# The mixer of a two-block fp32 model: one activation table set for exponential and logarithm, output maps ahead of head 0's sum, three copies on ScalarE, unread matmuls taken out

## The reference, cut to what matters

```python
# branch 1: a diagonal complex state-space model ("s5"), 32 groups of 16 channels, 64 states each
a_bar = exp(lam * dt)
bu = einsum('bsgc,gpc->bsgp', ug, b_bar)          # complex
states = scan(x_t = a_bar * x_{t-1} + bu_t)
y = Re(C states) + D_skip * u                     # later: gelu, gated linear unit
# branch 2: stick-breaking attention, 8 heads of 64
z = q.k / 8                                        # masked to s < t
log_fail = log_sigmoid(-z)                         # = -(max(z, 0) + log(1 + exp(-|z|)))
log_w = log_sigmoid(z) + (sum of log_fail between s and t)
w = exp(log_w);  out = w @ v
```

## Time and profile before

| | us |
|---|---|
| median of 3 runs | 1498.22 (1497.93 to 1499.45) |
| the profiled execution's own time | 1497.39 |
| its span, first to last instruction | 1495.6 |
| from the first chunk's `in_transposes` to the fourth's | 54.77 to 205.07 |
| busy in the span: PE, DVE, ACT | 1414.9, 955.8, 703.5 |

### The profile page before, as it was taken

How to read it: one execution, slowest core, us unless ns; L and a number is a source line. 1 busy time by engine, 2 the same in 40 slices (tenths; PEclk the granted TensorE clock), 3 DMA queues, 4 the chain that set the end, 5 groups by cost and what they waited for, 6 DMA issues and landing times.

```text
span 1495.6 us, 18290 instructions
## 1 busy us (share of the span) xinstructions
PE 1414.9 (95%) x7056; PEld 1190.4 (80%) x7056; DVE 955.8 (64%) x1333; ACT 703.5 (47%) x932; POOL 75.6 (5%) x82
## 2 busy tenths in 40 slices
PE   4899999999999999999979999999999999996996
PEld 3788887888888888888868889787878888885875
DVE  6898886444554444444469776546888778886474
ACT  4677767332342223222246444435456666565251
POOL 3000000000110000000020000020100000000211
PEclk9999999999999999999988999999999999997997
DMA  5111011322222232222311211322312111111211
GB/s 196 57 57 57 1 57 57 113 85 89 108 85 102 96 112 85 97 99 85 110 63 54 84 56 60 124 85 85 116 56 82 56 56 56 56 60 67 85 57 56
DMA packets 19242, 118.22 MB, mean 79 GB/s; under 512 B 2401, under 2 KB 3681, under 8 KB 5617
## 3 DMA queue, kind: packets, MB, share of 16 engines
q1 hardware_dynamic: 18896, 116.38, 21.8%
q0 software_dynamic: 288, 1.05, 0.2%
HBM read 115.32 MB, written 2.10 MB: 79 GB/s over the span
## 4 chain that ended last, share of the span: by engine, by line
PE 76%; DVE 13%; ACT 8%; issue 2%; DMA 0%; DVEq 0%; ACTq 0%
PE ps L508 23%; PE ps L510 23%; PE ps L509 23%; DVE wlo L1637 2%; PE ps L975 1%; PE ps L698 1%; PE ps L944 1%; DVE att L1894 1%; DVE acc L384 1%; ACT att L1217 1%; PE ps L579 1%; DVE atlo L1898 1%; PE ps L962 1%; ACT att L1215 1%; ACT att L1213 1%
## 5 line engine op out<-in xcount | busy, mean ns | idle before, releaser
L508 PE MATMUL ps<-uhi,whi 128*128 128x512 f32 x1104 | 442.5, 401 | 8.4 <-DVE ulo L1698 3.0
L510 PE MATMUL ps<-uhi,wlo 128*128 128x512 f32 x1104 | 433.1, 392 | 0.0
L509 PE MATMUL ps<-ulo,whi 128*128 128x512 f32 x1104 | 432.9, 392 | 0.0
L1637 DVE TENSOR_TENSOR wlo<-wraw,whi 128x2048 fp32r<-128x2048 f32 x105 | 243.5, 2321 | 103.1 <-ACT whi L1088 101.6
L1088 ACT ACTIVATE whi<-wraw 128x2048 fp32r<-128x2048 f32 x105 | 200.3, 1908 | 178.8 <-PE ps L510 178.4
L508 PEld LDWEIGHTS ps<-uhi,whi 128*128 128x128 f32 x1104 | 209.3, 190 | 56.6 <-issue 9.6
L510 PEld LDWEIGHTS ps<-uhi,wlo 128*128 128x128 f32 x1104 | 209.3, 190 | 45.4
L509 PEld LDWEIGHTS ps<-ulo,whi 128*128 128x128 f32 x1104 | 209.6, 190 | 43.6 <-issue 1.9
L508 PE MATMUL ps<-hdhi,whi 128*128 128x512 f32 x256 | 99.6, 389 | 0.0
L509 PE MATMUL ps<-hdlo,whi 128*128 128x512 f32 x256 | 99.6, 389 | 0.0
L510 PE MATMUL ps<-hdhi,wlo 128*128 128x512 f32 x256 | 99.6, 389 | 0.0
(11 more groups left out here) (405 smaller groups left out, 2484.1 us busy)
## 6 DMA issues: line engine op xcount, KB each, us to landing
wraw<-wstream SPq DMA_DIRECT2D x105, 1024.0 KB, 4.8
h<-xT SPq DMA_DIRECT2D x4, 512.0 KB, 5.7
outT<-pp SPq DMA_DIRECT2D x8, 256.0 KB, 2.2
s5b<-s5p_d SPq DMA_DIRECT2D x1, 1024.0 KB, 12.0
pe_in<-pT POOLq DMA_DIRECT2D x2, 512.0 KB, 3.8
cst_in<-cst_d SPq DMA_DIRECT2D x5, 64.0 KB, 10.1
reset<-cst_d SPq DMA_DIRECT2D x1, 256.0 KB, 11.1
ones<-cst_d SPq DMA_DIRECT2D x1, 64.0 KB, 2.1
```

The costliest lines, as they stand in the source:

```text
L508: nc.tensor.matmul(out, lh, rh, start=start, stop=False, skip_group_check=True)
L509: nc.tensor.matmul(out, lh, rl_, start=False, stop=False, skip_group_check=True)
L510: mm = nc.tensor.matmul(out, ll, rh, start=False, stop=stop, skip_group_check=True)
L1637: V.tensor_tensor(wlo[:, slot, :], wraw[:, slot, :], whi[:, slot, :], ALU.subtract).then_inc(lo_done, 1)
```

## The change

Four edits, all in the mixer:

1. `table` ends with an explicit load of the set that holds both exponential and logarithm. No other ACT_TABLE_LOAD stands between it and the next chunk's Sin.
2. `tokens`, the copy of y into `tT` (now `y_tokens`) and `decays` go from VectorE to ScalarE. Their waits and the semaphores that they signal stay the same.
3. `out_maps` comes first in VectorE's part of a chunk, with three independent passes at its head; `blocks` stands inside it, behind the fourth pass.
4. `keep_on` and its twelve matmuls a chunk are gone.

```diff
@@ TensorE
-            def keep_on(n, bank, moving):
-                for _ in range(n):
-                    nc.tensor.matmul(ps[:, bank, :], identr[:, :], moving, start=True, stop=True)
...
                 gemm(n, 0, one(0), 256, uhi, ulo)
                 block_sums()
-                keep_on(12, 1, uhi[:, 0, :])
                 log_weights(0)
@@ ScalarE
                 A(cosT[:, :, :], cosT[:, :, :], ACT.Sin, scale=-TWO_PI, bias=halfpi_b).then_inc(table_ready, 1)
+                nc.scalar.preload_act_table_set("natural_log_exp_and_others")
+            def tokens(i):
+                act.wait_ge(u_tr, i + 1)
+                copy(tT[:, :, :].rearrange("p q (j c) -> p j q c", j=L),
+                     ps[:, 1, :].rearrange("p (j q c) -> p j q c", j=L, q=QP)).then_inc(u_tok, 1)
+            def y_tokens(i):
+                act.wait_ge(y5_done, i + 1)
+                copy(tT[:, :, :].rearrange("p b (q c) -> p q b c", q=QP),
+                     ps[:, 6, :].rearrange("p (q b c) -> p q b c", q=QP, b=L)).then_inc(y_tok, 1)
+            def decays(i):
+                if i == 0:
+                    act.wait_ge(s5_exp, 3)
+                else:
+                    act.wait_ge(z5_done, i)
+                copy(decay[:, :, 1:], s5p[:, 10, QP * i:QP * i + QP].unsqueeze(2).to_broadcast([P, QP, NB - 1])).then_inc(
+                    decay_gen, 1)
...
                 log1p(0)
+                decays(i)
                 fail_hi(0)
...
                 split_hi(None, 0, i + 2, i * 4 + 6)
+                y_tokens(i)
                 weights(1)
...
                     in_evac(i + 1)
+                    tokens(i + 1)
@@ VectorE
             def out_maps(i):
+                dve.wait_ge(in_gen, i + 1)
                 if i >= 1:
                     dve.wait_ge(y5_done, i)
                 own.do(V.tensor_tensor(H[:, 0, :, :, :], matrix(i, 2, L + 1), powers(i, 0, 0, L + 1), ALU.mult))
                 own.do(V.tensor_tensor(tmp[:, :, :, :], matrix(i, 3, L + 1), powers(i, 0, 1, L + 1), ALU.mult))
+                own.do(V.tensor_tensor(H[:, 1, :, :, :], matrix(i, 3, L + 1), powers(i, 0, 0, L + 1), ALU.mult))
                 own.sync()
                 step(V.tensor_tensor(H[:, 0, :, :, :], H[:, 0, :, :, :], tmp[:, :, :, :], ALU.add))
-                own.do(V.tensor_tensor(H[:, 1, :, :, :], matrix(i, 3, L + 1), powers(i, 0, 0, L + 1), ALU.mult))
+                blocks(i)
                 own.do(V.tensor_tensor(tmp[:, :, :, :], matrix(i, 2, L + 1), powers(i, 0, 1, L + 1), ALU.mult))
...
-                decays(i)
-                blocks(i)
                 out_maps(i)
                 softplus(0)
...
                     k_lo(i + 1)
-                dve.wait_ge(y5_done, i + 1)
-                V.tensor_copy(tT[:, :, :].rearrange("p b (q c) -> p q b c", q=QP),
-                              ps[:, 6, :].rearrange("p (q b c) -> p q b c", q=QP, b=L)).then_inc(y_tok, 1)
                 split_lo(2 * i + 4, 0)
...
                     values_lo(i + 1)
-                    tokens(i + 1)
```

More of the change, by code:

```diff
@@ L1581, in _ @@
             in_evac(0)
+            tokens(0)
             for i in range(HC):
@@ L1790, in out_maps @@
                 V.tensor_tensor(H[:, 1, :, :, :], H[:, 1, :, :, :], tmp[:, :, :, :], ALU.subtract).then_inc(out_gen, 1)
[L1792 to L1799, removed]
             def phase(i):
@@ L1833, in values_lo @@
                                 ALU.subtract).then_inc(v_ready, 1)
[L1835 to L1839, removed]
             def blocks(i):
@@ L2313, in _ @@
             values_lo(0)
-            tokens(0)
             for i in range(HC):
```

## The result

The changed kernel takes 1483.91 us (median of 4 runs, 1481.55 to 1485.49) against 1498.08 for the kernel before on the same chip (4 runs, 1497.07 to 1499.45). The ratio is 0.9905 (95% interval 0.9894 to 0.9917), 14.2 us less. The prediction said 1482.9, 15.3 less, with a range of 1480.5 to 1485.8. The time lies in the range, 1.0 above the forecast. The interval of the ratio allows a gain of 12.4 to 15.9 us.

A forecast was written before the change was run, and what follows sets the result against it. TensorE bounds the program on average, but a mixer chunk is bound by its chain of waits over ScalarE and VectorE. Three chunks at 4.00 plus 3.28 give 15.28 off 1498.22: 1482.9 us, range 1480.5 to 1485.8.

The forecast's parts named there:

- Head 0's loads: Each mixer chunk, ScalarE ahead of softplus(0): two removed table loads, 1.30 us each, start softplus(0) 2.60 us earlier.
- The sum: Whole mixer: 4.00 us saved in each of chunks one to three, 3.28 in the fourth, 15.28 in all.
- rival (B): Ahead of softplus(0): a load costs more than its row, 0.5 us more a chunk, 1480.8 us; chance 0.05.
- Head 1's load: Each chunk ahead of softplus(1): ScalarE comes 1.30 us earlier, but VectorE becomes the limit, so 0.68 us pays.
- The copy of y: Copy into tT leaves VectorE's unbroken run to ET for ScalarE: 0.72 us in each of chunks one to three.
- Terms put at nothing: Mixer: moved tokens and decays copies, new load ahead of uch, Exp and Ln from the joint set cost nothing.
- The waits forecast at 0.9 and 0.68: TensorE's idle time in a changed chunk: 0.9 us ahead of log_weights(0), 0.68 ahead of y.
- Rival (A): Mixer chunks: only head 0's loads pay, a wait held for covered replaces the others; 1487.8 us; chance 0.12.
- The thinnest margin: Ahead of in_transposes: TensorE's side comes at most 4.09 us earlier, VectorE's 4.00, so VectorE still decides.
- taking them out is worth nothing by itself: Twelve unread matmuls ahead of log_weights(0): removal alone gains nothing, but is worth about 2 us to this edit.
- Rival (C): Behind log_weights(0): without fillers TensorE's clock falls; over half the stretch, 7.1 us, 6.4 a chunk lost, 1508; chance 0.04.
- a stretch of the mixer under 1.00: Sign of being wrong: granted clock below 1.00 in any mixer stretch, where the forecast expected 1.00.

The follow-up runs named there:

- ytok_on_vector: The changed kernel with the copy of y into tT back on VectorE; 1485.20 us, 0.9920 of the kernel before.
- maps_behind: The changed kernel with the old order of the output maps, block copy first, then all six passes; 1496.03 us, 0.9992 of the kernel before.
- two_sets: The changed kernel without the explicit load of the joint table set, all else as changed; 1501.80 us, 1.0024 of the kernel before.
- before_no_fillers: The kernel before with only the twelve unread matmuls of each chunk taken out; 1505.40 us, 1.0038 of the kernel before.
- before_again: The kernel before, unchanged, measured and traced once more; 1497.36 us, 0.9999 of the kernel before.

## Why the prediction was right, and where it was not

**Head 0's loads, 2.60 a chunk.** Measured 2.55: `softplus(0)` starts 7.22 us behind `in_transposes` (112.24 - 105.02) where it started 9.77 behind. This settles the price of a load as well. Each load paid 1.28, its own length: Exp now starts 1.28 behind Abs (2.56 before) and Ln 1.31 behind Exp (2.59 before). The sum's 1.30 also counted the hand-over of 0.02, which stays between any two passes. The Trainium skill (page "ScalarE: Activation LUTs", section "What ACT_TABLE_LOAD costs") adds a drain of about the load's own length. Had there been one on this chain, the removal of two would have moved `softplus(0)` until the maps held it, 0.91 further, and no idle time would be left ahead of it. The trace does not agree with the page, and rival (B) fell with it.

**Head 1's load, 0.68.** `y` starts 26.39 us behind `in_transposes` instead of 29.63, 3.24 for the two heads (forecast 3.28). `softplus(1)` has no idle time and starts 0.58 behind the moment that ScalarE would have allowed, so VectorE is the limit there, as forecast.

**The copy of y, 0.72.** Measured 0.60 as the rest of 3.84, and 0.58 in `ytok_on_vector`. This is the mis-sized term. Its 0.72 was read as start to start in the kernel before, and 0.11 of it was lost again ahead of `ys`, which starts 0.72 behind the last phase pass instead of 0.61.

**Terms put at nothing.** `tokens` and `decays` took 0.59 and 0.61 where 0.60 was assumed, `uch` kept 0.24 us of cover (0.5 by the sum), `w_lo(1)` kept 0.59 between the end of `athi` at 139.64 and its start at 140.23 (0.4 forecast), and Exp and Ln take 1.28 and 1.37 from the joint set. The waits forecast at 0.9 and 0.68 came out at 0.69 and 0.70. No run puts `tokens` or `decays` back alone; that they cost nothing is read from these rows. Rival (A), that one of these margins fails, did not happen.

**The thinnest margin was not thin.** The prediction left TensorE 0.09 us of wait ahead of `in_transposes` (4.09 against 4.00); it is 0.48. It took TensorE's work from `y` on to have no waiting in it. But `transpose_values` starts 19.06 behind `y` in the kernel before (153.56 - 134.50) and 18.79 in the changed one (150.20 - 131.41), and nearly all of these 0.27 lie where `weigh_values(1)` begins, which before came 0.15 behind the end of `atlo` (145.67 and 145.52) and now comes 0.69 behind it (142.41 and 141.72). So TensorE's side came about 3.5 earlier, and VectorE decided with room to spare.

**The sum.** At full clock 3 x 3.84 + 3.25 = 14.8 against the 15.28 predicted; the median says 14.2. The profiled execution alone gained 1497.39 - 1485.49 = 11.9, chiefly because its first chunk was partly at the low clock and that of the kernel before was not. The steps of the sum came out one by one, and that is no luck. That the median ended within 1.0 us of the forecast is partly luck: stretches that the change does not touch differ by 1.6 us (ahead of the mixer, without filled gaps) and 6 us (behind it) between executions.

**A sentence that was wrong,** though nothing in the sum hung on it: "taking them out is worth nothing by itself". On the kernel before it costs 6.7 us. The prediction costed the fillers by TensorE's order of waits alone; their absence also changes the clock. Rival (C) had the mechanism right and the price of its extreme too high. In the later chunks a fall behind the wait costs 1.0 to 1.6 us (`maps_behind`, `two_sets`, `before_no_fillers`), not 6.4, and in `two_sets` it lasts less than the four microseconds shown above, not the 7.1 of work that (C) supposed. In the first chunk of `two_sets` and `before_no_fillers` it lasts about twice as long and costs an estimated 2.3 to 2.6 (what those chunks lose beyond the 2.7 of the fall at their start). That it did not come in the changed kernel is due to the other edits: they shrink the wait from 3.23 to 0.69 us. With the maps behind (2.52) or with two sets (3.23) it came, though not in every chunk.

**The clock in the first chunk.** The prediction named a stretch of the mixer under 1.00 as a sign of being wrong, and the profiled execution has one, 0.94 in the first chunk. The clock of 1.00 in the later chunks was forecast rightly; that the first chunk's gap of 3.4 us mostly brings a fall was not, since one trace showed it without. It does not tell against the change's mechanism, because the kernel before has the same fall in `before_again`. The Trainium skill (page "TensorE: Matmul & The Clock Gate", section "Why this matters for your kernels") warns of idle gaps between bursts of matmuls. By that rule a kernel's fillers are not free to take out, and `before_no_fillers` agrees with it: a wait of 3.23 us, and a clock of 0.97 in the chunk instead of 1.00.

## What to carry to other kernels

Removing work from a chain pays up to the next engine's arrival and no further, so each removal needs the second-latest arrival as well; here the joint set alone gave 1.4 us a chunk, and 3.2 once the maps and the fillers were out of its way. Matmuls that nobody reads may be holding TensorE's clock: before taking them out, read how long the engine then waits at their place, and expect nothing from it while that wait is long. Edits that cover one another must be timed together, for apart they can even have the other sign.

## What the runs showed of the hardware that was not expected

- Whether an idle stretch of TensorE is followed by 1.2 GHz varies between executions of one kernel: behind 3.2 to 3.5 us ahead of the first chunk the clock fell in nine profiles of eleven, and stayed at 1.00 in two. It varies between chunks of one execution too: behind 3.24 us in the fourth chunk it fell in `before_no_fillers` and not in `two_sets`, and behind 2.52 us in two chunks of `maps_behind` out of four. A single trace can't show that a gap is harmless. Behind waits of 1.6 us and less inside the chunks no profile shows a fall.
- Time at 1.2 GHz behind the mixer was between 38.6 and 60.4 us in the fourteen profiles, and the same code there took 1234.1 us with the least of it and 1240.3 us with the most. With such differences one pair of profiles can't prove a few microseconds.
